# RWKV core: the block inverse in a mirrored form on four array quarters, with a new order of the 16 beats

## The reference, cut

```python
def rwkv7_branch(rw, mu, w0, w2, a0, a2, g2, k_k, k_a, r_k, ln_w, ln_b):
    ...
    def step(state, inp):
        r_t, w_t, k_t, v_t, kk_t, b_t = inp
        sk = jnp.einsum('bhvk,bhk->bhv', state, kk_t)
        state = (state * w_t[:, :, None, :] - sk[..., None] * b_t[:, :, None, :]
                 + v_t[..., None] * k_t[:, :, None, :])
        return state, jnp.einsum('bhvk,bhk->bhv', state, r_t)
    ...
    _, o = lax.scan(step, s0, (seq_first(r_h), seq_first(w_h), seq_first(k_h), seq_first(v_h),
                               seq_first(kk), seq_first(kk * a_h)))
    ...
    o = head_norm(o, RWKV_LN_EPS).reshape(b, s, wd) * ln_w.astype(F32) + ln_b.astype(F32)
    bonus = jnp.sum(r_h * k_h * r_k.astype(F32).reshape(RWKV_HEADS, RWKV_HEAD), axis=-1, keepdims=True) * v_h
    o = o + bonus.reshape(b, s, wd)
    return (o * gate).astype(out_dtype)
```

## Time and profile before

| | |
|---|---|
| median of 3 runs | 3146.2 us (3142.13 to 3154.13) |
| the profiled execution | 3149.86 us, span 3147.7 us |
| PE busy | 2949.8 us, 94% of the span, 22150 matmul records |
| DVE, ACT, POOL busy | 1545.0, 587.9, 865.7 us |
| mean granted PE clock | 0.979 |

### The profile page before, as it was taken

How to read it: one execution, slowest core, us unless ns; L and a number is a source line. 1 busy time by engine, 2 the same in 40 slices (tenths; PEclk the granted TensorE clock), 3 DMA queues, 4 the chain that set the end, 5 groups by cost and what they waited for, 6 DMA issues and landing times. The chain is left out here.

```text
span 3147.7 us, 52360 instructions
## 1 busy us (share of the span) xinstructions
PE 2949.8 (94%) x22150; PEld 2057.6 (65%) x22150; DVE 1545.0 (49%) x2520; ACT 587.9 (19%) x1102; POOL 865.7 (28%) x591
## 2 busy tenths in 40 slices
PE   9999999998999889999999998999878898999998
PEld 6855856896887678757566686677767744443433
DVE  5764746336465466544777664764544332111112
ACT  2142040003000433211000002221443311110101
POOL 1121122111121445211799791011255310000000
PEclk9999999999999899999999999999999999999999
DMA  4342223221331000032344453132200017999996
GB/s 165 93 164 71 89 81 113 74 74 41 115 94 53 3 3 4 36 129 79 120 128 145 145 167 90 57 94 80 68 16 3 22 70 279 372 409 409 409 409 267
DMA packets 122230, 412.64 MB, mean 131 GB/s; under 512 B 13568, under 2 KB 21376, under 8 KB 121744
## 3 DMA queue, kind: packets, MB, share of 16 engines
q1 hardware_dynamic: 112784, 373.64, 33.6%
q0 software_dynamic: 9216, 35.66, 3.5%
HBM read 404.97 MB, written 4.28 MB: 130 GB/s over the span
## 5 line engine op out<-in xcount | busy, mean ns | idle before, releaser
L947 PE MATMUL ps<-arena 128*128 128x256 f32 x4760 | 1044.4, 381 | 18.0 <-PEq L905 6.8
L947 PEld LDWEIGHTS ps<-arena 128*128 128x128 f32 x4760 | 898.8, 191 | 174.0 <-issue 43.9
L1003 PE MATMUL ps<-arena 128*128 128x512 f32 (+1 forms) x752 | 291.6, 546 | 10.4 <-DVE arena L1342 7.3
L885 POOL TENSOR_TENSOR arena<-arena 128x512 f32<-128x512 f32 x68 | 94.2, 1385 | 557.1 <-DVE arena L903 190.5
L1003 PEld LDWEIGHTS ps<-arena 128*128 128x128 f32 x752 | 144.3, 193 | 149.7 <-issue 139.0
L3936 PE MATMUL ps<-arena 128*64 128x512 f32 x1024 | 224.9, 594 | 10.6 <-DMA arena<-in_w_up 8.2
L891 POOL TENSOR_TENSOR arena<-arena 128x512 f32<-128x512 f32 x68 | 86.4, 1270 | 484.2 <-PE ps L947 484.2
L1247 DVE TENSOR_TENSOR arena<-ps,arena 128x256 f32<-128x256 f32 x85 | 36.1, 425 | 331.0 <-PE ps L947 330.0
L1178 DVE SCALAR_TENSOR_TENSOR arena<-ps,params,arena 128x511 f32<-128x511 f32 (+4 forms) x266 | 190.7, 717 | 13.5 <-ACT arena L1079 4.4
L4080 POOL TENSOR_SCALAR arena<-arena,small 128x1024 f32<-128x1024 f32 x64 | 191.3, 2989 | 11.5 <-DMA arena<-in_w_mod 7.9
L3936 PEld LDWEIGHTS ps<-arena 128*64 128x64 f32 x1024 | 83.7, 137 | 150.3 <-issue 149.8
(11 more groups left out here) (459 smaller groups left out, 4001.6 us busy)
## 6 DMA issues: line engine op xcount, KB each, us to landing
arena<-in_w_in SPq DMA_DIRECT2D x166, 512.0 KB, 3.7
arena<-in_w_gate SPq DMA_DIRECT2D x128, 512.0 KB, 15.4
arena<-in_w_up SPq DMA_DIRECT2D x128, 512.0 KB, 15.3
arena<-in_w_down SPq DMA_DIRECT2D x128, 512.0 KB, 15.4
arena<-in_w_mod POOLq DMA_DIRECT2D x48, 512.0 KB, 4.3
arena<-in_ffn_up SPq DMA_DIRECT2D x44, 512.0 KB, 4.0
arena<-in_w_branch SPq DMA_DIRECT2D x32, 512.0 KB, 3.6
arena<-spill POOLq DMA_DIRECT2D x16, 640.0 KB, 5.6
```

The lines of the kernel that those rows point to most:

```text
L885: vec.tensor_tensor(plane(u, n), part(u, 1, 0), part(u, 1, 1), ALU.add).then_inc(sem, 1)
L947: last = nc.tensor.matmul(k.bank(b)[:, 0:HT], lhs[:, q * P:(q + 1) * P], rhs[:, q, :], start=(first and q == 0), stop=(q == 3), skip_group ...
L1003: last = nc.tensor.matmul(out[0:j["m"], 0:j["n"]], w[:, q * m:(q + 1) * m], j["rhs"](q), start=(n == 0), stop=(n == kn - 1))
```

## The change

**Mirrored levels.** The full L is now also made transposed (`LS`, a second product in `step_lt`, 16 matmuls more), and the masks are `levelTC`. A level is now Y = (LM)'XT, XT = XT - X'Y and X = X - Y'X. Y is kept in a "turned" layout, in which the two halves of the partitions stand for heads instead of chunks, and so is X. Thereby X0, Y and XT are written by `to_heads` and `to_chunks`, which go round all four quarters and fill banks 0 and 1 together; X alone stays on two quarters (`in_heads`), in bank 6. Y5 and XT5 use the same helpers on banks 2 and 3. The number of steps is the same, 13 in A and 12 in B, each of 16 matmuls or 4 transpositions as before. DVE writes L in three instructions as before, and each A and B step is still read out by one instruction, from two banks where it was one.

**New order.** In A, XT comes before X, since Y of the next level now needs XT. Beats are listed by hand in `A_BEAT` and `B_BEAT`. `trv` and `trkap` exchange banks and `Lk` comes before `XT5`; `NU0` follows `WT`, `Ab` precedes `Ak`. L is made in beat 14 (13 before). On DVE the centring of O is in beat 0 (1), the scan of `prepare` in beat 1 (0), the variance in beat 2 (4); on POOL the products move to later beats (8 and 11 instead of 6 and 8), the normalisation to an earlier one. `elif` became `if`, so that several of these may share a beat. Since X uses bank 6, waits are added between X and the users of that bank.

```diff
-    A = ["X0"] + [f"{s}{n}" for n in (1, 2, 3, 4) for s in ("Y", "X", "XT")]
-    B = ["trv", "Y5", "trkap", "XT5", "Lk", "trkt", "LkV", "trbt", "NU0", "WT", "Ak", "Ab"]
-    B_BEAT = [0, 0, 2, 2, 3, 4, 5, 6, 6, 7, 9, 11]
-    B_BANKS = [(3,), (2,), (3,), (2,), (2, 3), (3,), (2,), (3,), (2,), (2, 3), (2, 3), (2, 3)]
-    LT_BEAT = 13
+    A = ["X0"] + [f"{s}{n}" for n in (1, 2, 3, 4) for s in ("Y", "XT", "X")]
+    B = ["trv", "Y5", "Lk", "XT5", "trkt", "trkap", "LkV", "trbt", "WT", "NU0", "Ab", "Ak"]
+    B_BEAT = [0, 1, 1, 2, 4, 4, 5, 6, 7, 8, 10, 12]
+    B_BANKS = [(2,), (2, 3), (2, 3), (2, 3), (2,), (3,), (2,), (3,), (2, 3), (2,), (2, 3), (2, 3)]
+    X_BANK = 6
+    A_BEAT = [1, 3, 4, 4, 5, 6, 7, 8, 11, 11, 13, 15, 15]
+    LT_BEAT = 14
+    TURN_BEAT, WEIGHED_BEAT, BONUS_BEAT, ADDED_BEAT = (9, 8), (10, 10), (13, 12), (14, 13)
...
-    a_steps = lambda beat: A[beat * len(A) // 16:(beat + 1) * len(A) // 16]
+    a_steps = lambda beat: [s for s, t in zip(A, A_BEAT) if t == beat]
...
-            def blocks64(l, r, b):
-                for h in range(2):
+            def to_heads(l, r, b):
+                for i in range(TT):
+                    for q, h in ((0, 0), (1, 1), (0, 1), (1, 0)):
+                        other = k.const("ident")[half(q), half(q)] if r is None else r[half(q), cell(h, i)]
+                        ins = nc.tensor.matmul(k.bank(b + q)[half(h), 64 * i:64 * i + 64], l[half(q), cell(h, i)], other, start=True, stop=True)
+                return ins
+
+            def to_chunks(l, r, b):
+                for i in range(TT):
+                    for h, q in ((0, 0), (1, 1), (0, 1), (1, 0)):
+                        t = turned_cell(q, i)
+                        ins = nc.tensor.matmul(k.bank(b + h)[half(q), 64 * i:64 * i + 64], l[half(h), t], r[half(h), t], start=True, stop=True)
+                return ins
+
+            def in_heads(l, r, b):
+                for q in range(2):
                     for i in range(TT):
-                        for q in range(2):
-                            other = k.const("ident")[half(q), half(q)] if r is None else r[half(q), cell(h, i)]
-                            ins = nc.tensor.matmul(k.bank(b)[half(q), cell(h, i)], l[half(q), cell(h, i)], other, start=True, stop=True)
+                        for h in range(2):
+                            t = turned_cell(q, i)
+                            ins = nc.tensor.matmul(k.bank(b)[half(h), t], l[half(h), t], r[half(h), t], start=True, stop=True)
                 return ins
...
                 elif s[0] == "Y":
-                    n = int(s[1:])
                     pe.wait_ge(lm_ok, 4 * p + n)
-                    pe.wait_ge(*a_out(p, f"X{n - 1}"))
-                    ins = blocks64(LM(p), X(p), b)
+                    pe.wait_ge(*a_out(p, f"XT{n - 1}" if n > 1 else "X0"))
+                    ins = to_heads(LM(p), XT(p), 0)
                 elif s[:2] == "XT":
-                    pe.wait_ge(*a_out(p, "Y" + s[2:]))
-                    ins = blocks64(Y(p), XT(p), b)
+                    pe.wait_ge(*a_out(p, f"Y{n}"))
+                    if n > 1:
+                        pe.wait_ge(*a_out(p, f"X{n - 1}"))
+                    ins = to_chunks(X(p), Y(p), 0)
                 else:
-                    pe.wait_ge(*a_out(p, "Y" + s[1:]))
-                    if s != "X1":
-                        pe.wait_ge(*a_out(p, f"XT{int(s[1]) - 1}"))
-                    ins = blocks64(XT(p), Y(p), b)
+                    pe.wait_ge(*a_out(p, f"Y{n}"))
+                    if n == 1:
+                        pe.wait_ge(kap_ok, min(p + 2, PAIRS))
+                        if p >= 1:
+                            pe.wait_ge(*a_out(p - 1, "X4"))
+                    else:
+                        pe.wait_ge(*a_out(p, f"X{n - 1}"))
+                    if p >= 3 and n == 3:
+                        pe.wait_ge(weighed, p - 2)
+                    if p >= 3 and n == 4:
+                        pe.wait_ge(bonus_ok, p - 2)
+                    ins = in_heads(Y(p), X(p), X_BANK)
...
-                products(pl(a + p), pl(sg + p), 2).then_inc(lt_made, 1)
+                products(pl(a + p), pl(sg + p), 2)
+                products(pl(sg + p), pl(a + p), 2, 256).then_inc(lt_made, 1)
...
-                nc.vector.tensor_tensor(quad(LT(p)), two_banks(2), mask(strict), ALU.mult).then_inc(lt_read, 1)
+                nc.vector.tensor_tensor(quad(XT(p)), two_banks(2), mask(first_level), ALU.mult)
+                nc.vector.tensor_tensor(quad(LS(p)), two_banks(2, 256), mask(after), ALU.mult).then_inc(lt_read, 1)
                 dve.wait_ge(lt_read, p + 1)
-                link(nc.vector.scalar_tensor_tensor(out=eight(XT(p)), in0=eight(LT(p)), scalar=-1.0, in1=mask8(level(0)), op0=ALU.mult, op1=ALU.mult))
-                nc.vector.tensor_tensor(eight(XT(p)), eight(XT(p)), mask8(ident), ALU.add).then_inc(lt_out, 1)
+                nc.vector.tensor_tensor(eight(XT(p)), mask8(ident), eight(XT(p)), ALU.subtract).then_inc(lt_out, 1)
```

More of the change, by code:

```diff
@@ L2104, in rwkv_core_phase @@
     b_made_at = lambda p, s: p * len(B) + B.index(s) + 1
+    last_user = lambda bank: [s for s, banks in zip(B, B_BANKS) if bank in banks][-1]
     def users_before(s):
@@ L2386, in step_a @@
                 act.wait_ge(a_made, a_made_at(p, s))
-                nc.scalar.activation(Y(p) if s[0] == "Y" else X(p), k.bank(A.index(s) % 2), ACT.Copy).then_inc(a_act, 1)
+                nc.scalar.activation(pair(Y(p) if s[0] == "Y" else X(p)), both(0), ACT.Copy).then_inc(a_act, 1)
             def step_b(p, s):
@@ L2395, in step_b @@
                     ins = nc.scalar.activation(NU(p), src, ACT.Copy, scale=-1.0)
+                elif s == "Y5":
+                    ins = nc.scalar.activation(pair(Y(p)), both(2), ACT.Copy)
                 else:
-                    dst = {"Y5": Y(p), "trv": VT(p), "trkap": KAPT, "trkt": KT_(p), "trbt": BT_(p), "LkV": LKV}[s]
+                    dst = {"trv": VT(p), "trkap": KAPT, "trkt": KT_(p), "trbt": BT_(p), "LkV": LKV}[s]
                     ins = nc.scalar.activation(dst, src, ACT.Copy)
@@ L2540, in step_b @@
                     dve.wait_ge(*a_out(p, "XT4"))
-                    ins = nc.vector.tensor_tensor(XT(p), XT(p), k.bank(2), ALU.subtract)
+                    ins = nc.vector.tensor_tensor(pair(XT(p)), pair(XT(p)), both(2), ALU.subtract)
                 elif s == "WT":
```

103 lines of the change are left out of this document (59 added, 44 removed).

## The result

The changed kernel takes 3116.48 us in the median (3114.29 to 3122.56, 4 runs), the one before on the same chip 3146.45 (3142.13 to 3154.13, 4 runs): a ratio of 0.9904, 95% interval 0.9889 to 0.9919, or 30 us less. The profiled execution took 3118.1 (span 3116.0).

A forecast was written before the change was run, and what follows sets the result against it. PE was taken to set the pace, with DVE next. Block savings summed to -37 us at full clock, +4 for the clock gave -33, so 3113 us on the median of 3146.2; range 3102 to 3130.

The forecast's parts named there:

- The case that I thought likeliest: Whole phase: shorter steps, trkt stall gone, smaller waits instead; -33 us, 3113 us, own range 3103 to 3122, chance 0.68.
- The price of a step: PE's A and B steps: 0.95 us on two quarters, 0.5 on four; eleven change, full-block work 30.5 to 26.1.
- The waits: PE idle in a full block: trkt's 2.39 us goes, new waits for ACT and DVE come, 4.0 us in all.
- The 0.5, 0.65 and 0.45: PE idle: chunk_u for the state in beat 2, XT5 for Lk's banks, state 6 behind nu6 in beat 13.
- The clock: PE's clock after idle: one half of blocks 3 to 8 lose 1.4 us, +4 us in all.
- Reading two banks: DVE and ACT reads: no extra cost on DVE, 0.6 us on ACT, as for one bank.
- Blocks 1 and 2: First blocks of the phase: 22.1 us becomes about 19.3, and 25.9 becomes 21.0.
- Block 9 and the tail: End of phase: block 9 saves 0.9 but pays for serial banks, 23.6 to 24.1 us; tail unchanged at 55.
- The clock's: Rival: each of blocks 3 to 8 drops clock for twice as long, 13 us instead of 4; 3122 us, chance 0.12.
- The second: Rival: PSUM reading bounds, PE waits for DVE in later beats, full block 33 us; +17, 3130 us, chance 0.10.
- The third: Rival: alternating banks or turned operands keep steps at 0.95 us, so nothing is saved; 3146 us, chance 0.05.
- POOL's: Rival: POOL's normalised O comes 10 us late against 2.2 slack and holds PE at swap; 3163 us, chance 0.05.

The follow-up runs named there:

- e5: Changed kernel with one POOL product (r times kk, 1.27 us) issued twice in blocks that finish a pair; 3116.6 us.
- e9: Changed kernel with one old number back, ACT's first exponential of the decay in beat 1 instead of 2; 3143.1 us.
- e1: Changed kernel with the same to_heads and to_chunks matmuls and banks, but only two quarters alternating at a time; 3124.8 us.
- v1 to v5: Four variants of the changed kernel that move Lk, the variance, or variance and norms' spread, against PE's two waits; 3114.7, 3118.0, 3116.5 and 3116.8 us.
- e6: Changed kernel with DVE's reduction of O (0.72 us) issued twice in beat 0 of blocks that finish a pair; 3119.6 us.
- e4: Changed kernel without the second product for L (16 matmuls a pair fewer, values not the reference's); 3111.8 us.
- v4: Changed kernel with the variance in beat 4 and PE's norms' spread moved between Y5 and Lk; 3116.5 us.

## Why the prediction was right

The forecast was 3113, the time 3116.5. The forecast sum of 33 us was a sum over the phase, and the phase gave 28.7; that the whole of the profiled executions gave 31.8 is in part luck, since 3.0 of it lie where nothing was changed. The case that I thought likeliest is the one that came, with its mechanism: shorter steps, the stall at trkt gone, smaller waits in its place. But its sum is right with parts that are not, and that their errors cancel is luck. Against the forecast of 37 us at full clock, blocks 1 and 2 gave 6.2 too little, block 3 1.3 (28.5 for 27.2), block 8 1.0 (27.3 for 26.3), block 9 with the tail 1.8, and the four full blocks 1.9 too much (118.6 for 120.5); 4 of these 37 had been set aside for the clock.

- **The price of a step**: right. to_heads takes 0.69 us for 32 records in the rows where it stands by itself at full clock. The drop of PE's work as a whole is smaller than forecast. I had 30.5 to 26.1, 4.4 a block at full clock. In the three full blocks at clock 1.00 PE is busy for 27.44, 27.70 and 27.10, so 26.1 was 1.0 to 1.6 short; which steps hold the rest is open. Before, over the four full blocks, it was 31.4 at clock 0.96, and after 27.8: 3.7 less with the clock's part in it.
- **The waits**: total too large, 4.0 forecast and 1.8 measured a block (9.2 marked over five blocks), 0.5 of it of a kind I did not have. Lk for ACT's copy of Y5: 0.9 forecast, 0.73 to 0.77 measured. State before the second chunk_u: 1.5 forecast, 0.23, 0.27, 0.87 and none in the four full blocks. The 0.5, 0.65 and 0.45 did not come. The term that failed is DVE in beats 0 to 2: I carried 1.14 for the centring and 1.55 for the scan over from the old order, where they ran beside POOL, though the change moves POOL's first product from beat 1 to beat 3. They take 0.69 and 1.23. That is 0.8 us off DVE's chain by the second chunk_u and XT5, a part of what those waits came out shorter by; the rest I can't assign. The two errors, over the four full blocks PE busy 1.7 a block more than the 26.1 (0.4 of it the clock of one block) and idle 2.1 less than the 4.0, left 29.65 against 30.1. The Trainium skill, page "SBUF — State Buffer", Who interferes with whom, has the port pair that DVE and GpSimd share as an exclusive lock. The rows agree with it in direction in both orders: 1.14 us beside POOL's product and 0.69 without, 1.60 and 1.23.
- **The clock**: too dear. Half of blocks 3 to 8 were to lose 1.4 us; in the profile one of them, block 7, shows less than 1.00 (0.94, with 28.79 busy against 27.10, so up to 1.7 us). That one isn't told by its idle: block 7 has a single piece of 0.75 us, until 1212.14, and the granted clock then stands at 0.50 to 0.52 from 1215 to 1218, while block 6 with 0.77 and 0.87 keeps 1.00.
- **Reading two banks**: 0.60 us on ACT, as taken, and 0.69 on DVE.
- **Blocks 1 and 2**: the largest miss. Block 1 was to give 2.8 and block 2 4.9. Block 1 gave 2.0, which a later start took back: the first product of L begins 1.4 us later and X0 2.1 us later, the clock being at its lower level (0.50) there. How much of that is the change's is open: in e5, the same code there, X0 starts at 1042.9, ahead of the 1045.5 of before, and its block 1 takes 19.8 us from X0 on, as here. Block 2 took 24.4 and not 21.0. For it I gave a length and named no wait; PE's timeline has seven, 4.9 us together, among them:

```profile
1069.05 0.70 PE L2162 MATMUL ps<-cst,arena 64*64 64x64 f32 x32 [0.76 <-DVE arena L2576]
1070.99 0.69 PE L2148 MATMUL ps<-arena 64*64 64x64 f32 x32 [0.78 <-ACT arena L2437]
...
1090.15 0.34 PE L2148 MATMUL ps<-arena 64*64 64x64 f32 x6 [1.28 <-issue]
```

- **Block 9 and the tail**: from the start of block 9 to the next phase it took 78.6 us before and 80.9 after, 2.3 more where 0.5 were forecast. The tail, from the first gate product on, has 57.3 for 55.7 of it, with the clock at 0.97 there; block 9 up to that product 23.5 for 22.9.
- **Rivals.** The clock's did not come in the changed kernel, but e9 shows that it was real: waits of 3 us and more a block went with as much again in longer records. The second (DVE's reads) came in part: not 33 us a block, but DVE's order shares the bound, so that e1 costs 1.0 a block for 2.8 of longer steps and v1 to v5 gain nothing. The Trainium skill's page "TensorEngine Tiling (Array Packing)", PSUM Bottleneck, had it that the reading of PSUM may become the limit of a tiled engine. Here it is not the reading of two banks that costs (0.69 on DVE, as for one), but DVE's order in the first beats: the readers that PE waits for stand behind the scan, the centring or the variance. The third is out by the 0.69. POOL's is out by e5: a product more is free, at least 1.27 of the slack of 2.2 is there.
- **What the prediction did not see** is how much stands on the new beats. I took them as the frame of my replay. With the old ones the same inverse gains 10 us, and a single exponential ahead of two copies takes 26.6 back. Had the change kept that one number, my steps for the pace would have stood and the time been 3143, 30 us above the forecast.

What stays open: how much of the 30 us the pace of four quarters is by itself, the share of e6's 4.6 us that DVE's longer queue made, and what the second product for L costs. Moving the scan or the differences out of beats 0 and 1 was not tried.

## What to carry to other kernels

When steps get shorter on the bound engine, replay the first few handoffs of a block with every instruction of the other queues in its new place, and look at what stands ahead of each copy that frees a bank: here one activation that waited for another engine was worth nearly the whole change. Take durations for the replay from rows with the same neighbours: here a scan and a centring measured beside a POOL product took 0.4 us longer than without one. And where a wait goes away only because an instruction was moved into the next gap, look for it there: four such moves gained nothing here. Whether work taken out of the first beats altogether would gain was not tried.

## What the runs showed of the hardware

**Quarters and banks give a step three paces.** 32 records of 64x64 f32 take 1.15 us in the old steps (two diagonal quarters in turn, both writing one bank), 0.98 when two diagonal quarters write two banks and the other two follow, and 0.69 when all four are visited in turn. The first two differ in the bank and not in which quarters alternate; no run takes the two apart any further. The text on the kernel before says that two row halves may not write one bank. The old steps do write one bank from both, in different partitions, at 1.15.

**A wait can have a second price in the clock.** In e9 waits of 3.05 to 3.87 us in each full block went with a granted clock of 0.90 over the five blocks and 11.7 us of longer records; with idle pieces under 1 us in the changed kernel the clock was 0.99. Short pieces are not safe in every block: in block 7 it stood at 0.50 to 0.52 for 3 us, as told above, with 0.75 us of idle in the whole block.

**Idle pieces of PE that nothing releases.** They are absent in the five blocks before and come with the faster steps: 2.5 us in the changed kernel, 0.9 in e1 with its slower steps, up to 5.1 in others. In the profiles of all the kernels with the new inverse but e4 one stands at the same place of the program, ahead of the last 14 records of a step of X in block 5, and lasts 0.50 to 1.05 us (PE's timeline of the changed kernel):

```profile
1173.41 0.68 PE L2177 MATMUL ps<-arena 64*64 64x64 f32 x14 [0.78 <-issue]
```

A fixed place in the program and no engine that releases it speak for the delivery of instructions. The instruction queue's row of the DMA view over 146 us (packets, MB, share), before and then after:

```profile
q8 instruction: 29, 0.48, 1.4%
```

```profile
q8 instruction: 36, 0.59, 1.7%
```

The row alone says little, since PE has more records in the same window after, 4439 against 3684. That cause is argued; no run took it away.

**Small DVE instructions beside POOL.** With the variance in beat 4 (v4) its second instruction ran beside two POOL products and took 0.61 us where it takes 0.17 in block 6 of the changed kernel. A reduction over 128x512 is not longer there (0.67, and 0.69 in the changed kernel). DVE, then POOL:

```profile
1187.21 0.61 DVE L2654 TENSOR_SCALAR small<-small 128x8 f32<-128x8 f32 x1
```

```profile
1186.52 2.50 POOL L2504 TENSOR_TENSOR arena<-arena 128x512 f32<-128x512 f32 x2 [1.14 <-issue]
```
